# A decoder trunk on one core: another order for the first stage's table strips, weight splits and sums of squares

## What is computed

```python
mods = (silu(c) @ w_ada + b_ada).reshape(B, N_MOD, D_MODEL)     # N_MOD = 16, w_ada is 1024 x 16384
h = rmsnorm(x, g) * (1 + scale) + shift                         # shift, scale: the first two of mods
a = h @ w_pw1 + b_pw1                                           # 1024 -> 2048
u = a[..., :D_MODEL] * sigmoid(a[..., D_MODEL:])
y = depthwise_conv(u, w_dw, width 31) + b_dw
y = silu(layernorm(y, ln_g, ln_b)) @ w_pw2                      # 1024 -> 1024
x = x + gate * y
```

## Time and profile before

| | |
|---|---|
| median of three runs | 1843.25 us |
| the profiled execution, its own time | 1838.12 us |
| its span | 1836.5 us |
| TensorE busy | 1669.3 us, 91% |
| VectorE busy | 874.1 us, 48% |
| ScalarE busy | 620.7 us, 34% |
| GpSimd busy | 211.7 us, 12% |
| moved by the DMA engines | 198.17 MB, mean 108 GB/s |
| chain that ended last, by engine | TensorE 76%, VectorE 10%, "issue" 5%, ScalarE 5%, DMA 2% |

### The profile page before, as it was taken

How to read it: one execution, slowest core, us unless ns; L and a number is a source line. 1 busy time by engine, 2 the same in 40 slices (tenths; PEclk the granted TensorE clock), 3 DMA queues, 4 the chain that set the end, 5 groups by cost and what they waited for, 6 DMA issues and landing times.

```text
span 1836.5 us, 31217 instructions
## 1 busy us (share of the span) xinstructions
PE 1669.3 (91%) x12897; PEld 1480.9 (81%) x12897; DVE 874.1 (48%) x1613; ACT 620.7 (34%) x1197; POOL 211.7 (12%) x289
## 2 busy tenths in 40 slices
PE   5899977979999999979898999988879999999994
PEld 3677755979999999978898844554779999999994
DVE  3599996452333232362234277566363233223333
ACT  4455456332221222232213456454333221122212
POOL 1013220300000000002100254323100000000000
PEclk8899988989999999988999999788989999999997
DMA  9698865523332333313312310100232332223311
GB/s 307 212 312 305 285 227 163 143 57 103 113 110 67 95 95 112 93 47 86 82 47 79 121 34 20 47 24 24 70 92 62 89 98 77 68 81 88 100 33 52
DMA packets 236534, 198.17 MB, mean 108 GB/s; under 512 B 7202, under 2 KB 195954, under 8 KB 236128
## 3 DMA queue, kind: packets, MB, share of 16 engines
q1 hardware_dynamic: 229744, 172.25, 30.9%
q0 software_dynamic: 6352, 23.88, 4.3%
q10 hardware_dynamic: 304, 0.10, 0.0%
HBM read 188.88 MB, written 11.20 MB: 109 GB/s over the span
## 4 chain that ended last, share of the span: by engine, by line
PE 76%; DVE 10%; issue 5%; ACT 5%; DMA 2%; DVEq 1%; POOL 1%; SPq 0%; ACTq 0%; POOLq 0%
PE ps L1594 60%; PE ps L1574 4%; PE ps L1960 2%; PE ps L1913 2%; PE ps L1839 1%; DVE wl L1075 1%; PE ps L1606 1%; DVE y L1266 1%; DVE r L1266 1%; DMA ada<-in_w_ada_dram 1%; DVE r L1083 1%; DMA xrows<-in_x_sample_dram 1%; PE ps L1630 1%; PE ps L2030 1%; PE ps L1625 1%
## 5 line engine op out<-in xcount | busy, mean ns | idle before, releaser
L1594 PE MATMUL ps<-Hh,wh 128*128 128x288 f32 x2128 | 467.4, 302 | 50.5 <-DVE Hl L1116 32.1
L1594 PE MATMUL ps<-Hl,wh 128*128 128x288 f32 x2128 | 462.0, 299 | 0.0
L1594 PE MATMUL ps<-Hh,wl 128*128 128x288 f32 x2128 | 461.4, 299 | 0.0
L687 ACT ACTIVATE wh<-raw 128x1024 fp32r<-128x1024 f32 (+1 forms) x173 | 192.8, 1117 | 780.0 <-PE ps L1594 778.4
L1594 PEld LDWEIGHTS ps<-Hh,wh 128*128 128x128 f32 x2128 | 348.5, 192 | 59.6 <-issue 57.1
L1594 PEld LDWEIGHTS ps<-Hl,wh 128*128 128x128 f32 x2128 | 348.6, 192 | 0.2
L1594 PEld LDWEIGHTS ps<-Hh,wl 128*128 128x128 f32 x2128 | 348.2, 191 | 0.2
L1075 DVE TENSOR_TENSOR wl<-raw,wh 128x1024 fp32r<-128x1024 f32 (+1 forms) x173 | 223.7, 1294 | 252.1 <-ACT wh L687 251.6
L1594 PE MATMUL ps<-al,wh 128*128 128x288 f32 x704 | 150.8, 296 | 0.0
L1594 PE MATMUL ps<-ah,wl 128*128 128x288 f32 x704 | 150.7, 296 | 0.0
L1594 PE MATMUL ps<-ah,wh 128*128 128x288 f32 x704 | 150.7, 296 | 0.0
(11 more groups left out here) (294 smaller groups left out, 1930.1 us busy)
## 6 DMA issues: line engine op xcount, KB each, us to landing
ada<-in_w_ada_dram SPq DMA_DIRECT2D x64, 1024.0 KB, 8.0
raw<-in_ffn_w_up_dram SPq DMA_DIRECT2D x88, 512.0 KB, 3.8
raw<-in_ffn_w_down_dram SPq DMA_DIRECT2D x32, 704.0 KB, 4.5
raw<-in_conv_w_pw_dram SPq DMA_DIRECT2D x24, 512.0 KB, 9.3
raw<-in_w_kv_dram SPq DMA_DIRECT2D x12, 512.0 KB, 3.8
C<-in_cache_kv_dram POOLq DMA_DIRECT2D x32, 128.0 KB, 4.3
out_win_sample_dram<-in_state_win_dram POOLq DMA_DIRECT2D x8, 512.0 KB, 3.8
raw<-in_nsa_w_in_dram SPq DMA_DIRECT2D x8, 512.0 KB, 3.8
```

Source lines behind the costliest of these rows:

```text
L687: A(wh[:, u % RING, 0:K, 0:w], raw[:, u % RING, 0:K, 0:w], ACT.Copy).then_inc(hi_ready, 1)
L1594: last = M(ps[0:w, 2 * s + h, 0:HT], wt[:, s, k, 0:w], rt[:, k, h * HT:(h + 1) * HT], start=(k == 0 and i == 0), stop=(k == K - 1 and i == 2))
```

## The change

It changes six things. The rest of the program is word for word the same.

1. **Squares.** ScalarE squares four chunks, copies out strip 0, and then squares the other four. VectorE adds in two levels, so that TensorE gets 2 chunks to sum where it got 4; the copies of the small vectors (L1165 to L1167) stand between the two fours.
2. **Order around the root.** ScalarE writes strip 0 and splits unit 0 before the root, writes strip 1 and splits unit 1 behind it, and then does all of strip 2. VectorE splits unit 0 before the reciprocal. TensorE turns strip 2 before the first product instead of inside it.
3. **Inside the first product.** Strip 3's second half stands before it; strip 3's turn stays at chunk 1; block 5 is turned at chunk 4 instead of 5, strip 4's halves stand at chunk 6 and behind the product (chunks 5 and 7 before). ScalarE copies out block 5 before the first sigmoid.
4. **Behind the first product.** Block 6 follows at once and unit 2 after it: the turn of strip 4 and the whole of strip 5 that stood before unit 2 are gone from there (`STRIPS_AHEAD` 1 for 2, and 2 for 1 in the plan at unit 2).
5. **Splits.** VectorE splits unit 2 before the first sigmoid, unit 3 behind it, and unit 4 after the third tap.
6. **Layer norm.** One strip less before it (`STRIPS_TAIL` 2 for 3), and two (`STRIPS_LN` 2 for 1), both behind the sums of squares; ScalarE's part of them is behind the root, and in the second projection its calls come one step later.

```diff
-STRIPS_AHEAD = 2
-STRIP_PLAN = [0, 0] + [1, 2] * 7
-STRIPS_TAIL, STRIPS_LN, STRIPS_PW2 = 3, 1, 1
+STRIPS_AHEAD = 1
+STRIP_PLAN = [0, 0, 2, 2] + [1, 2] * 6
+STRIPS_TAIL, STRIPS_LN, STRIPS_PW2 = 2, 2, 1
...
# SyncE
-            strips(10)
+            strips(11)
...
# ScalarE
-            square0(0, DC)
+            square0(0, 4)
             strip_out(0, None)
+            square0(4, DC)
+            strip_out(1, None)
             act.wait_ge(S("vec_dve"), 3)
+            strip_out(None, 0)
+            split_hi(0)
             root(0)
-            strip_out(1, 0)
             strip_out(None, 1)
-            for u in range(2):
-                split_hi(u)
+            split_hi(1)
+            strip_out(2, None)
+            strip_out(None, 2)
...
+            norm0_smp(0)
             norm0_hi(0)
-            strip_out(3, 2)
+            norm0_hi(1)
+            strip_out(3, None)
+            norm0_hi(2)
             strip_out(None, 3)
-            norm0_hi(1)
+            norm0_hi(3)
+            split_hi(2)
+            norm0_smp(1)
+            for cc in range(4, DC):
+                norm0_hi(cc)
+            for h in range(2):
+                block_out(5, h)
...
                     if u == 1:
-                        split_hi(2)
+                        split_hi(3)
                         strip_out(s_, None)
-                        for bk in (5, 6):
-                            block_out(bk, 0)
-                            block_out(bk, 1)
-                        strip_out(s_ + 1, s_)
-                        s_ += 2
-                        split_hi(3)
+                        for h in range(2):
+                            block_out(6, h)
+                        s_ += 1
...
             sample_out(DC - 1)
-            strip_out(s_ + 2, s_ + 1)
...
                 A(sqb[:, cc, :], y[:, cc, :], ACT.Square).then_inc(S("ln_sq"), 1)
-                if cc == 1:
-                    strip_out(s_, s_ - 1)
-                    s_ += 1
             act.wait_ge(S("ln_pe"), 2 * DC - 2)
             A(halves(r[:]), stats0, ACT.Sqrt, scale=1.0 / D, bias=epst[:]).then_inc(S("ln_rms"), 1)
+            strip_out(s_, s_ - 1)
+            s_ += 1
...
# VectorE
+            for cc in (0, 4):
                 dve.wait_ge(S("st_sq"), cc + 2)
+                add_squares(cc, cc + 1)
+                dve.wait_ge(S("st_sq"), cc + 4)
+                add_squares(cc + 2, cc + 3)
+                dve.wait_ge(S("st_a0"), 3 * (cc // 4) + 2)
+                add_squares(cc, cc + 2)
...
+            split_lo(0)
             dve.wait_ge(S("st_rms"), 1)
             V.reciprocal(r[:], r[:]).then_inc(S("st_r"), 1)
-            for u in range(2):
-                split_lo(u)
+            split_lo(1)
...
             norm0(1)
+            split_lo(2)
...
-                if j == 0:
-                    split_lo(2)
-                    split_lo(3)
-                split_lo(ua + 1 + SPLIT_AHEAD)
+                split_lo(ua + SPLIT_AHEAD if j == 0 else ua + 1 + SPLIT_AHEAD)
...
+                if j == 0:
+                    split_lo(ua + 1 + SPLIT_AHEAD)
...
# TensorE
             strip_half(1, 0)
+            strip_half(1, 1)
-            for cc in range(0, DC, 2):
-                pe.wait_ge(S("st_a0"), cc // 2 + 1)
-                sum_chunk(sqb[:, cc, :], cc, S("st_c0"), DC - 1, bank=4)
-            strip_half(1, 1)
+            pe.wait_ge(S("st_a0"), 3)
+            sum_chunk(sqb[:, 0, :], 0, S("st_c0"), DC - 3, bank=4)
             pe.wait_ge(S("vec_dve"), 3)
             turn_strip(0)
+            pe.wait_ge(S("st_a0"), 6)
+            sum_chunk(sqb[:, 4, :], 4, S("st_c0"), DC - 3, bank=4)
+            turn_strip(1)
             strip_half(2, 0)
-            turn_strip(1)
             strip_half(2, 1)
             strip_half(3, 0)
+            turn_strip(2)
+            strip_half(3, 1)
...
             def first_strips(k):
                 if k == 1:
-                    turn_strip(2)
-                    strip_half(3, 1)
-                elif k == 2:
                     turn_strip(3)
-                elif k == 5:
+                elif k == 4:
+                    block_in(5)
+                elif k == 6:
                     strip_half(4, 0)
-                    block_in(5)
-                elif k == 7:
-                    strip_half(4, 1)
...
             dense(0, Hh, Hl, normed0, tiles=2, ahead=first_strips)
+            strip_half(4, 1)
             block_in(6)
-            turn_strip(STRIPS_FIRST)
-            strip(STRIPS_FIRST + 1)
...
```

More of the change, by code:

```diff
@@ L706, in root @@
                 A(scrap[:], epst[:], ACT.Sqrt).then_inc(S("st_tb"), 1)
-                act.wait_ge(*((S("st_ck"), sums_done(st)) if st else (S("st_c0"), DC // 2)))
+                act.wait_ge(*((S("st_ck"), sums_done(st)) if st else (S("st_c0"), 2)))
                 A(halves(r[:]), stats if st else stats0, ACT.Sqrt, scale=1.0 / D, bias=epst[:]).then_inc(S("st_rms"), 1)
@@ L768, in _, with norm0_smp, norm0_hi @@
             act.wait_ge(S("xi_act"), 5)
-            square0(0, DC)
+            square0(0, 4)
             strip_out(0, None)
+            square0(4, DC)
+            strip_out(1, None)
             act.wait_ge(S("vec_dve"), 3)
+            strip_out(None, 0)
+            split_hi(0)
             root(0)
-            strip_out(1, 0)
             strip_out(None, 1)
-            for u in range(2):
-                split_hi(u)
-            def norm0_hi(q):
+            split_hi(1)
+            strip_out(2, None)
+            strip_out(None, 2)
+            def norm0_smp(q):
                 act.wait_ge(S("n0_s"), 3 * q + 3)
                 A(Hh[:, 4 * q:4 * q + 4, TP:T], fs[:, 4 * q:4 * q + 4], ACT.Copy).then_inc(S("n0_hi"), 1)
-                for cc in range(4 * q, 4 * q + 4):
-                    act.wait_ge(S("n0_t"), cc + 1)
-                    A(Hh[:, cc, 0:TP], t2[:, cc % 2, 0:TP], ACT.Identity, bias=mods[:, cc, 0:1]).then_inc(S("n0_hi"), 1)
-            strip_out(2, None)
+            def norm0_hi(cc):
+                act.wait_ge(S("n0_t"), cc + 1)
+                A(Hh[:, cc, 0:TP], t2[:, cc % 2, 0:TP], ACT.Identity, bias=mods[:, cc, 0:1]).then_inc(S("n0_hi"), 1)
+            norm0_smp(0)
             norm0_hi(0)
-            strip_out(3, 2)
+            norm0_hi(1)
+            strip_out(3, None)
+            norm0_hi(2)
             strip_out(None, 3)
-            norm0_hi(1)
+            norm0_hi(3)
[5 more added lines that the diff above has]
+                block_out(5, h)
             def sample_rows(j):
@@ L872, in _ @@
                 square(1, m)
-                if m < STRIPS_PW2:
+                if m <= STRIPS_PW2:
                     strip_out(s_, s_ - 1)
                     s_ += 1
-                elif m == STRIPS_PW2:
+                elif m == STRIPS_PW2 + 1:
                     strip_out(None, N_STRIP - 1)
@@ L1758, in _ @@
             convs += 1
-            next_strip()
             pe.wait_ge(S("cs_ev"), DC)
@@ L1769, in _ @@
                 sum_chunk(sqb[:, cc, :], cc, S("ln_pe"), 7, bank=4)
+            for _k in range(STRIPS_LN):
+                next_strip()
             def ln_ready(cc):
```

14 lines of the change are left out of this document (7 added, 7 removed).

## The result

The changed kernel takes **1830.22 us** (median of 16 runs, 1822.85 to 1832.66); the kernel before took 1841.68 beside it (16 runs, 1833.18 to 1844.16). The ratio is 0.994, with a 95% interval of 0.9927 to 0.9952: 9 to 13 us faster. The forecast was 1826 between 1820 and 1836, a gain of 16.9; what came is 11.5 by the medians. The profiled execution of the changed kernel took 1830.03 of its own, that of before 1838.12, so the two traces show 8.1 of the 11.5: the execution of before lies 3.6 under its median.

A forecast was written before the change was run, and what follows sets the result against it. VectorE's taps bound the loop and TensorE everything behind the second projection's start, so earlier gains pass through: 12.3 to layer norm + 5.6 in it - 1.0 = 16.9; 1843.25 - 16.9 = 1826.3, range 1820 to 1836.

The forecast's parts named there:

- signs of being wrong altogether: A loop start later than 80, or a time behind the projection that differs from before by more than 2.
- Root and first product: First stage: first half norm at 38.7 (2.0 earlier), first product 43.5 (1.3 earlier), second half norm 54.1 (1.4 earlier).
- The first pair's end: Second half norm's start to the first sigmoid takes 12.2 for 14.4; sigmoid at 66.3, 3.5 earlier.
- Behind the pair: After the first sigmoid: unit 2 at 70.3, loop 14.2 earlier at 72.5, second sigmoid 92.6 to 93.3, losing 0.4.
- Rival A: Strips starve the loop: TensorE waits for w_ada halves, layer norm begins only 6 to 9 earlier; 1833 or 1830; chance 0.13.
- Lead: In the loop TensorE's lead over VectorE starts from nothing, then grows; layer norm can begin 12.3 earlier.
- TensorE's chain: From the last sigmoid through strips, copies, sample convolutions and sums of y to layer norm: the later chain by 1.5.
- Layer norm: End of the taps to second projection: 2.2 + 8.2 + 7.9 + 1.2 = 19.5 for 25.1, 5.6 earlier.
- rival B: Layer norm gives its part back: TensorE rests between the sums, six chunks 4.6 later; 1831; chance 0.09.
- Second projection: Strip 31's product waits for strip 30's row, which ScalarE copies behind its first square: 1.0 later.

The follow-up runs named there:

- run with the taps held: Changed kernel with GpSimd's first product for the sample rows' taps held back until the second half norm is written: 1825.6, ratio 0.9907.
- copies early: Changed kernel with those GpSimd taps held and VectorE's 16 copies put before the first half norm's last low part: 1819.95, ratio 0.9865.
- all together: Changed kernel with GpSimd's taps held, the 16 copies early and one layer norm strip before the sums of squares: 1818.02, ratio 0.986.
- filled: Changed kernel with five matmuls, whose result nobody reads, between the last sum of y and the sums of squares: 1827.61, ratio 0.9922.
- strip-between run: Changed kernel with one of its two layer norm strips between the last sum of y and the sums of squares: 1826.1, ratio 0.9905.

## Why the prediction was right, and where it wasn't

The time lies within the range, 4.2 over the forecast of 1826, and the mechanism held in kind: the order was late, not the work. In size it held less well than the time suggests: at strip 31 the traces show 7.1 of the 16.9, under half. Its signs of being wrong altogether didn't show: the loop starts at 77.26 and not later than 80, and behind the projection both traces take 1527.1. By its own steps:

- *Root and first product.* 38.7, 43.5 and 54.1 forecast, 39.73, 43.90 and 54.57 measured. The 1.0 at the first comes with the lower clock near 25, which the forecast's sums (2.7 for two, measured 2.29 and 2.27 each) don't have. The table load cost its 1.28 and no more, as the row of before had it. Strip 3's turn did come earlier as laid out; it moved from chunk 2 to chunk 1 (the list of the change has it staying at chunk 1). "Most of strip 3's gain is given to the copies" was right, and moving them away is worth 3.65 at the second half norm.
- *The first pair's end* is **the step that failed**: "from the second half norm's start to the sigmoid" 12.2, measured 16.7. The forecast priced the 16 copies on VectorE but not what they release: two operations of GpSimd that before fell into VectorE's wait and now fall on its next two rows, 1.7 and 1.6 of stretch. The run with the taps held brings 3.4 of the 4.5 back. The other 1.1 (13.3 against the 12.2 laid out) is the clock: in that run TensorE waits 2.75 for the second half norm and does the next 12 groups of products in 4.87, at 0.65; with the copies early it waits 1.14 and does them in 3.40, at 1.00, and there the same way takes 11.8.
- *Behind the pair.* Sigmoid to unit 2 was forecast at 4.0 and took 4.03; unit 2 to the second sigmoid 22.3 to 23.0, and took 24.2. The wait there is 2.49 for 0.4. The work there is as forecast; at full clock it took 22.52 (all together), within the forecast's bounds, and the lower clock behind the wait at 75.28 makes the rest. Rival A named the wait rightly and its cause mostly wrongly: a late half is 0.57 of it; for the rest TensorE is full, and slow at first.
- *Lead.* The 1.5 for TensorE's chain was not lost: TensorE waited 1.42 for the last `y` and not the other way round. These errors cancel, and that is luck: the wait is 2.1 more and the lead's loss 1.5 less, and the loop without its wait is 0.65 shorter than before. From the first sigmoid to E the forecast had 205.7, and 205.5 was measured. So the 4.7 that E is late are the first sigmoid's 4.95.
- *Layer norm* is the second step that failed: forecast 19.5, measured 24.55. Three terms: the last sum took 2.26 at the low clock and the mean came 3.12 behind E (2.2); the sums of squares ran at a granted clock of 0.64, 2.3 more, which is **rival B**, right in kind, at half its price of 4.6 (the other traces with this order of layer norm have 0.9 to 2.4); and the last half of w_ada came 2.60 late instead of the 1.2 "taken over", 1.9 more in this term. The filled and the strip-between run show the last two as causes.
- *Second projection.* The 1.0 at strip 31 came as forecast (0.98), and the strip-between run takes it away.

On the profiles, 16.9 loses 4.7 at E and 5.1 in layer norm, which leaves 7.1 at strip 31; the stretch behind it is 1.1 shorter, which makes the 8.1. The medians show 11.5, as the profiled execution of before was a quick one. Rivals A and B together were given 22 in 100, A at 3 to 6 us and B at 4.6. B came true at half its price; of A only the one late half did; and the largest loss, GpSimd's, is in no rival. The loss that the forecast allowed for in layer norm alone, a TensorE that comes out of a rest at the lower clock, came in three places: behind the second half norm, at unit 2, and in layer norm. That the measured time lies between the forecast and the two rivals is thus in part luck.

Not settled: what each of the first five parts of the change is worth, what the layer norm part is worth by itself, and how much of the 3.6 between the profiled execution of before and its median belongs to the first stage.

## What to carry to other kernels

When work that releases another engine is moved, follow the release: price what the released engine then runs beside, above all GpSimd beside VectorE operations with two SBUF inputs. Where a chain passes through an engine that rests between its steps, put there the filler that must be done anyway (here one strip), rather than behind the chain; a neat chain with rests in it ran slower than a filled one in the traces. Where a forecast takes a gap out or puts one in, look at the granted clock behind every gap of the bounding engine, and not only in the place where one expects it. And before one blames the loads for a wait, sum the bounding engine's own work in that stretch: moving requests earlier gained nothing, moving one strip away removed the wait, and the other chain then gave it back.

## What the runs showed of the hardware

- While a GpSimd `TENSOR_TENSOR` on 128x1024 runs, VectorE's `TENSOR_TENSOR` with two SBUF inputs takes five times as long, 2.16 and 2.06 for 0.42, and the second ends 0.28 behind GpSimd's own end. In the loop it is the other way round: VectorE's `SCALAR_TENSOR_TENSOR` rows stay at 0.74 and the GpSimd operation waits. Its eight executions in the changed kernel, as minimum, median and maximum in ns:

```profile
L572 POOL TENSOR_TENSOR taps<-sel,wd x8: 1957/3602/9506, 54.7 to 242.6; 128x1024 f32<-128x1024 f32 x8
```

- At the end of a group such an operation gets its turn, and VectorE's closing `TENSOR_TENSOR y<-y,r`, at 147.38 in the changed kernel, takes 2.49 instead of 0.69; GpSimd's row starts at 147.36.
- A table load of 1.28 on the path had 0.02 before it and 0.01 behind it. The Trainium skill (ScalarE: Activation LUTs, "What ACT_TABLE_LOAD costs") puts a drain of some 1.38 beside each switch; no run here shows one.
- The granted clock of TensorE was 0.50 in 275 to 280 of the changed kernel, across waits of 1.42 and 2.34, and 0.64 in the next ten; with products in that gap it was 1.00 in the same ten. Six chunks of sums cost 8.86 at the one and 6.15 at the other.
- The same wait of 2.1 was followed by the lower level in one execution and by the full one in another, with one program up to there: 12 groups of products took 4.91 or 3.39. So one trace's milestones carry a scatter of 1.5 for each such place.
